# A 512-column and a 256-column product per weight tile pair become three products of 256 columns, and the copy of the low half goes

## What is computed

```python
def first_block(...):
    mod = silu(c) @ w_ada + b_ada                     # six vectors: shifts, scales, gates
    h = modulate(rmsnorm(x, g_norm_mix), sh1, sc1)
    proj = h @ w_in                                   # 2048 -> 3072
    ...                                               # convolution, gated recurrence, pooling
    x = x + gt1 * (concat([y_lru, y_pool]) @ w_out)
    h = modulate(rmsnorm(x, g_norm_ffn), sh2, sc2)
    f = (silu(h @ w_ffn_gate) * (h @ w_ffn_up)) @ w_ffn_down     # 2048 -> 5632 -> 2048
    x = x + gt2 * f
    return rmsnorm(x, g_norm_final)

def second_block(x, ...):
    h = rmsnorm_2(x, attn_norm_w)
    proj = h @ w_in                                   # 2048 -> 11264
    ...                                               # retention and block attention
    merged = sigmoid(g_ret) * (o_ret @ w_ret_up) + sigmoid(g_moba) * (o_moba @ w_moba_up)
    x = x + merged @ w_out
    up = causal_dwconv_2(rmsnorm_2(x, ffn_norm_w) @ w_ffn_up, conv_w, conv_b)
    a, b = split(up, 2)
    x = x + (silu(a) * b) @ w_ffn_down
    return rmsnorm_2(x, final_norm_w)
```

## Time and profile before

| | |
|---|---|
| time, median of 3 runs | 2662.82 us (2662.07 to 2663.64) |
| span of the profiled execution | 2662.5 us |
| TensorE matmuls busy | 2521.5 us, 95%, 14020 instructions |
| weight loads busy | 2142.7 us, 80%, 14020 |
| VectorE busy | 1904.7 us, 72%, 2383 |
| ScalarE busy | 1183.1 us, 44%, 1437 |
| granted TensorE clock, mean | 0.995 |
| granted clock at half | 426.0 to 439.6 us, and from 2648.1 on |

### The profile page before, as it was taken

How to read it: one execution, slowest core, us unless ns; L and a number is a source line. 1 busy time by engine, 2 the same in 40 slices (tenths; PEclk the granted TensorE clock), 3 DMA queues, 4 the chain that set the end, 5 groups by cost and what they waited for, 6 DMA issues and landing times.

```text
span 2662.5 us, 38962 instructions
## 1 busy us (share of the span) xinstructions
PE 2521.5 (95%) x14020; PEld 2142.7 (80%) x14020; DVE 1904.7 (72%) x2383; ACT 1183.1 (44%) x1437; POOL 9.8 (0%) x37
## 2 busy tenths in 40 slices
PE   1399998999999999999999999999999999999997
PEld 0286676888888888888888888888888888888886
DVE  7899887865555555577677565576788758875886
ACT  1154434444444444464344455455544444444443
POOL 1000000000000000000000000000000000000000
PEclk9999998999999999999999999999999999999998
DMA  9888996965555555565555455565555555565553
GB/s 359 328 314 286 341 335 231 338 214 185 186 187 183 189 184 188 162 193 180 172 177 168 160 169 191 190 183 190 180 186 185 189 180 185 182 196 182 189 170 114
DMA packets 158485, 553.91 MB, mean 208 GB/s; under 512 B 18337, under 2 KB 22433, under 8 KB 158385
## 3 DMA queue, kind: packets, MB, share of 16 engines
q1 hardware_dynamic: 156384, 549.85, 60.8%
q0 software_dynamic: 848, 2.69, 0.3%
q10 hardware_dynamic: 1152, 0.03, 0.0%
HBM read 550.38 MB, written 2.10 MB: 208 GB/s over the span
## 4 chain that ended last, share of the span: by engine, by line
PE 89%; DVE 8%; issue 2%; ACT 1%; DMA 1%; DVEq 0%; SPq 0%; ACTq 0%
PE ps L499 54%; PE ps L501 27%; DVE acc L1104 4%; PE ps L494 2%; PE ps L496 1%; PE pm L534 1%; DVE split L1060 1%; PE pm L544 1%; DMA x_t<-in_x_fm 0%; ACT split L764 0%; DVE xc L1259 0%; DVE ssq L1141 0%; PE pm L649 0%; DVE val L1175 0%; PE pm L594 0%
## 5 line engine op out<-in xcount | busy, mean ns | idle before, releaser
L1060 DVE TENSOR_TENSOR split<-raw,split 128x1024 fp32r<-128x1024 f32 (+1 forms) x864 | 1032.3, 1203 | 660.4 <-ACT split L764 658.2
L764 ACT ACTIVATE split<-raw 128x1024 fp32r<-128x1024 f32 (+1 forms) x864 | 897.7, 1043 | 1205.0 <-PE ps L501 1106.0
L499 PE MATMUL ps<-h_s,split 128*128 128x512 f32 x3904 | 1383.6, 399 | 16.1 <-DVE h_s L1169 7.2
L501 PE MATMUL ps<-h_s,split 128*128 128x256 f32 x3904 | 1094.4, 280 | 0.0
L499 PEld LDWEIGHTS ps<-h_s,split 128*128 128x128 f32 x3904 | 734.8, 188 | 208.9 <-issue 20.0
L499 PE MATMUL ps<-mid_s,split 128*128 128x512 f32 x2368 | 836.9, 399 | 0.2 <-DVE split L1060 0.2
L501 PEld LDWEIGHTS ps<-h_s,split 128*128 128x128 f32 x3904 | 738.6, 189 | 0.5
L501 PE MATMUL ps<-mid_s,split 128*128 128x256 f32 x2368 | 663.5, 280 | 0.0
L499 PEld LDWEIGHTS ps<-mid_s,split 128*128 128x128 f32 x2368 | 444.8, 188 | 121.8 <-issue 12.1
L501 PEld LDWEIGHTS ps<-mid_s,split 128*128 128x128 f32 x2368 | 446.8, 189 | 0.0
L771 ACT ACTIVATE low<-ps 128x512 f32<-128x512 f32 x224 | 129.9, 580 | 4.4 <-PE ps L501 4.4
(11 more groups left out here) (222 smaller groups left out, 1155.2 us busy)
## 6 DMA issues: line engine op xcount, KB each, us to landing
raw<-in_w_in SPq DMA_DIRECT2D x224, 512.0 KB, 3.3
ride<-in_w_ada_late SPq DMA_DIRECT2D x128, 512.0 KB, 5.6
raw<-in_w_ffn_down SPq DMA_DIRECT2D x128, 512.0 KB, 3.3
raw<-in_w_ffn_gate SPq DMA_DIRECT2D x88, 512.0 KB, 3.3
raw<-in_w_ffn_up SPq DMA_DIRECT2D x88, 512.0 KB, 3.4
raw<-in_w_ffn_a SPq DMA_DIRECT2D x88, 512.0 KB, 4.1
raw<-in_w_ffn_b SPq DMA_DIRECT2D x88, 512.0 KB, 4.4
ada<-in_w_ada SPq DMA_DIRECT2D x64, 512.0 KB, 5.8
```

The lines of the kernel that those rows point to most:

```text
L499: pe.matmul(ps[:, s, b, :], split[:, slot, k, 0, b * P:(b + 1) * P], acts[:, k0 + k, :, :].rearrange("p h t -> p (h t)"), start=start, sto ...
L501: mm = pe.matmul(ps[:, s, b, 0:T], split[:, slot, k, 1, b * P:(b + 1) * P], acts[:, k0 + k, 0, :], start=False, stop=stop)
L764: act.activation(split[:, c, 0:kt, 0, :], raw[:, CHUNKS * s + c, 0:kt, :], ACT.Copy).then_inc(hi_ready, 1)
L1060: dve.tensor_tensor(split[:, c, 0:kt, 1, :], raw[:, CHUNKS * s + c, 0:kt, :], split[:, c, 0:kt, 0, :].bitcast(F32), ALU.subtract).then_inc ...
```

## The change

Each k-tile and block now has three matmuls of 256 columns, all onto `ps[:, s, b, 0:T]`: high × high, high × low (the high weight tile again), low × high. The second half of each PSUM bank is no longer used. `copy_low`, `last_turn`, the tile `low` and the semaphore `low_copied` go, and with them the waits of ScalarE for `evacuated`. The place of `low` in SBUF stays empty, so no address moves. `evacuate` waits for `chunk_used` itself, with the count of the slab's last chunk, and reads PSUM: a copy where nothing is scaled, one multiplication where it is by rows, two (one for each block) by columns. It has one step on VectorE's own semaphore less where it scales, thus `per` falls by two.

```diff
-    low = at("low", [P, 2, 2, T], place(2 * 2 * T * 4))
+    place(2 * 2 * T * 4)
...
                 for b in range(2):
-                    if tok:
-                        pe.matmul(ps[:, s, b, :], acts[:, k0 + k, 0, b * P:(b + 1) * P],
-                                  split[:, slot, k, :, :].rearrange("p h n -> p (h n)"), start=start, stop=False)
-                        mm = pe.matmul(ps[:, s, b, 0:SLAB], acts[:, k0 + k, 1, b * P:(b + 1) * P],
-                                       split[:, slot, k, 0, :], start=False, stop=stop)
-                    else:
-                        pe.matmul(ps[:, s, b, :], split[:, slot, k, 0, b * P:(b + 1) * P],
-                                  acts[:, k0 + k, :, :].rearrange("p h t -> p (h t)"), start=start, stop=False)
-                        mm = pe.matmul(ps[:, s, b, 0:T], split[:, slot, k, 1, b * P:(b + 1) * P],
-                                       acts[:, k0 + k, 0, :], start=False, stop=stop)
+                    block = slice(b * P, (b + 1) * P)
+                    for n, (w, x) in enumerate(((0, 0), (0, 1), (1, 0))):
+                        weight, act = split[:, slot, k, w, :], acts[:, k0 + k, x, :]
+                        left, right = (act[:, block], weight) if tok else (weight[:, block], act)
+                        mm = pe.matmul(ps[:, s, b, 0:T], left, right, start=start and n == 0, stop=stop and n == 2)
             mm.then_inc(chunk_used, 1)
...
-        def copy_low(E, s, used):
-
-            act.wait_ge(chunk_used, used)
-            if not (isinstance(E, int) and E < 2):
-                act.wait_ge(evacuated, E - 1)
-            act.activation(low[:, s, :, :], ps[:, s, :, T:2 * T], ACT.Copy).then_inc(low_copied, 1)
...
-            S = 2 * pair + s
-            copy_low(S + offset[0], s, CHUNKS * S + CHUNKS)
...
-        def evacuate(E, s, dst, scale=None):
-
-            dve.wait_ge(low_copied, E + 1)
-            both = low[:, s, :, :]
+        def evacuate(E, s, dst, used, scale=None):
+
+            dve.wait_ge(chunk_used, used)
             if scale is None:
-                ins = dve.tensor_tensor(dst, ps[:, s, :, 0:T], both, ALU.add)
+                ins = dve.tensor_copy(dst, ps[:, s, :, 0:T])
+            elif scale == "columns":
+                for b in range(2):
+                    ins = dve.tensor_scalar(dst[:, b, :], ps[:, s, b, 0:T], rstd_col[:, b:b + 1], None, ALU.mult)
             else:
-                own(dve.tensor_tensor(both, ps[:, s, :, 0:T], both, ALU.add))
-                if scale == "columns":
-                    for b in range(2):
-                        ins = dve.tensor_scalar(dst[:, b, :], both[:, b, :], rstd_col[:, b:b + 1], None, ALU.mult)
-                else:
-                    ins = dve.tensor_tensor(dst, both, scale[:, :].unsqueeze(1).to_broadcast([P, 2, T]), ALU.mult)
+                ins = dve.tensor_tensor(dst, ps[:, s, :, 0:T], scale[:, :].unsqueeze(1).to_broadcast([P, 2, T]), ALU.mult)
             ins.then_inc(evacuated, 1)
             dve.wait_ge(evacuated, E + 1)
...
-                per = 1 if first == S_FFN else 2 * (CONV_2 - 1) + 4
+                per = 1 if first == S_FFN else 2 * (CONV_2 - 1) + 2
```

More of the change, by code:

```diff
@@ L261, in build @@
     chunk_used = sem("chunk_used")
-    low_copied = sem("low_copied")
     evacuated = sem("evacuated")
@@ L764, in convert @@
             act.activation(split[:, c, 0:kt, 0, :], raw[:, CHUNKS * s + c, 0:kt, :], ACT.Copy).then_inc(hi_ready, 1)
-        def copy_low(E, s, used):
-            act.wait_ge(chunk_used, used)
-            if not (isinstance(E, int) and E < 2):
-                act.wait_ge(evacuated, E - 1)
-            act.activation(low[:, s, :, :], ps[:, s, :, T:2 * T], ACT.Copy).then_inc(low_copied, 1)
-        offset = [0]
         def turn(pair, s, mid=None, kt_next=KT):
@@ L783, in turn @@
                     mid(c)
-            S = 2 * pair + s
-            copy_low(S + offset[0], s, CHUNKS * S + CHUNKS)
-        def last_turn(pair, s):
-            S = 2 * pair + s
-            copy_low(S + offset[0], s, CHUNKS * S + CHUNKS)
         def turn_rows(S, c):
@@ L960, in ffn @@
                             square(n_sq, q - 1)
-                            last_turn((down + q) // 2, q % 2)
                     square(n_sq, OUT_SLABS - 1, pre)
@@ L1033, in _ @@
                     convert(pair + 1, 0, c)
-                if c == 1:
-                    copy_low(S_MERGE + 2 * m, 0, CHUNKS * (S_MERGE + m) + 2)
-            copy_low(S_MERGE + 2 * m + 1, 1, CHUNKS * (S_MERGE + m) + 4)
             act.wait_ge(merged_t, m + 1)
             act.activation(h_s[:, 2 * m:2 * m + 2, 0, :], val[:, 0, :, :], ACT.Copy).then_inc(merged_hi, 1)
-        offset[0] = OUT_SLABS
         pre_2 = (3, mid_s, col("ffn_norm_w_2", 0, DB))
@@ L1088, in turn @@
                     mid(c)
-            evacuate(2 * pair + s + offset[0], s, dst, scale)
+            S = 2 * pair + s
+            evacuate(S + offset[0], s, dst, CHUNKS * S + CHUNKS, scale)
         def add_ada(part, k, first, piece, loaded, times, added):
@@ L1400, in residual_turn @@
                 both(1)
-                evacuate(2 * pair + s + offset[0], s, val[:, s, :, :])
+                evacuate(2 * pair + s + offset[0], s, val[:, s, :, :], CHUNKS * (2 * pair + s) + CHUNKS)
             else:
@@ L1668, in _ @@
                         dve.wait_ge(merged_ready, m)
-                    evacuate(S_MERGE + 2 * m, 0, val[:, 0, :, :])
+                    evacuate(S_MERGE + 2 * m, 0, val[:, 0, :, :], CHUNKS * (S_MERGE + m) + 2)
                     own(dve.tensor_tensor(val[:, 0, :, :], val[:, 0, :, :], sig_r[:, 2 * m:2 * m + 2, :], ALU.mult))
-            evacuate(S_MERGE + 2 * m + 1, 1, val[:, 1, :, :])
+            evacuate(S_MERGE + 2 * m + 1, 1, val[:, 1, :, :], CHUNKS * (S_MERGE + m) + 4)
             own(dve.tensor_tensor(val[:, 1, :, :], val[:, 1, :, :], sig_m[:, 2 * m:2 * m + 2, :], ALU.mult))
```

## The result

| | before | after |
|---|---|---|
| time, median | 2663.2 us (2662.1 to 2664.9) | 2716.3 us (2714.6 to 2717.5) |
| ratio to before, 95% interval | | 1.0199 (1.0186 to 1.0212) |
| span of the profiled execution | 2662.5 us | 2715.7 us |

The change costs 53 us, 2.0%. The forecast was 2650; the range (2600 to 2775) holds the time, the direction was wrong. The time lies outside the likeliest case's own bounds (2610 to 2679); the range holds it because it was drawn round rival one's 2768.

A forecast was written before the change was run, and what follows sets the result against it. The prediction took the spacing of TensorE's matmuls as the bound: 2662.5 us, less 10.9 for TensorE and 1.5 for VectorE and ScalarE, gave 2650.1, stated as 2650, with a range of 2600 to 2775.

The forecast's parts named there:

- the likeliest case: Whole kernel: the forecast of 2650 us with the bounds of both its parts, 2610 to 2679; chance 0.50.
- rival one: Weight product on TensorE: every load costs a fixed 15.7 ns, a triple 367.2 ns, +107 us, 2768 us; chance 0.22.
- What bounds the kernel: Whole kernel: TensorE's matmul spacing sets the time, 89% of the chain; VectorE and ScalarE savings count only where TensorE waits.
- The TensorE part: Weight product: three 256-column steps of 116.6 ns, 349.9 for a pair's 351.5, -10.9 us over 6784; bounds -48 to +17.
- A load fits under a 256-column step: Weight product on TensorE: a load of 0.113 us hides under a 116.6 ns step with some 4 ns to spare.
- The slow supply: TensorE instruction supply: a load with its matmul due every 117 ns may come too slowly, 0 to +180 us; chance 0.05.
- Rival two: Weight product on TensorE: 256-column steps alone settle at the load's 0.113 us, a triple 339 ns, -85 us, 2576; chance 0.12.
- Rival three: TensorE's loop turns: larger bodies fetch instructions again, 1.4 us in each of 58 turns, +78 us, 2728 us; chance 0.06.
- Rival four: Weight product: the second load of the same high tile is left out, 349.9 ns a triple; no chance of its own.
- The VectorE and ScalarE parts: Evacuation and low copy: ScalarE loses 130 us, VectorE 60, nearly all off the path; -1.5 us, bounds -1 to -5.
- the cover: Each slab's evacuation: the 0.58 us low copy runs beneath a 1.2 us VectorE convert; if that failed, 130 us.
- The last down group: Before the last down products: TensorE waits 1.74 us for hidden values; one addition less gives back 0.68 us.

The follow-up runs named there:

- only the split: Kernel before with its 512-column product issued as two of 256, low copy and old evacuation kept: 2717.9 us, ratio 1.0198.

## Why the prediction was wrong, by its own steps

**What bounds the kernel: right.** The spacing of TensorE's matmuls set the time and little else counted.

**The TensorE part: the direction was lost here.** The step that failed is "I take what the trace shows of such a step: 3 × 116.6". The 116.6 ns was the recorded step of a 256-column matmul between 512-column ones. In a series of its own it is 120.0: 8.5 ns a triple more than the pair instead of 1.6 less, + 57.7 us where the sum had - 10.9. The error was to split a pair of 351.5 ns into two costs, 234.8 and 116.6, at the recorded start between them. The run with 384 + 128 + 256 columns shows that such a split can be off by 50 ns (170 for 120, 60 for 111.5). The two uniform series give the costs, 226.7 + 120.0 = 346.7 ns, and that is the pair of the faster rhythm (346.9); the slower rhythm adds 6.7 to it. The pair's mean of 351.5 is a mix of the two.

**"A load fits under a 256-column step": right, and no help.** The floor seen in series is 111.5 ns, and the one-column matmuls had shown it well enough (113). But 13.3 ns stand beside the columns although the floor lies under the step.

**Rival one came nearest, mis-sized.** It had a fixed time for every load; the runs show one for every matmul with its whole load, without telling which of the two has it. It said 15.7 ns, taken from the mean pair (31.5 / 2), and 2768 us. The faster rhythm (26.9 / 2 = 13.4, worked out in the same paragraph) was the right source: 13.3. Three of these and 320 ns of columns are 360.0, and with this the rival's own sum gives 2719 for the 2716 measured. Its own deciding point, a 256-column step over 117.5 ns, was met at 120.0. Both arguments against it fell. The excess of the 512-column step being twice that of the 256-column one came from the recorded split; in series of their own both have 13.3. And that the half clock shows no excess is true and says nothing of the upper clock; after the change the row is

```profile
440.61 3.62 PE L496 MATMUL ps<-h_s,split 128*128 128x256 f32 x16
```

(3.62 - 0.41) / 15 = 0.214 us, the bare columns at 1.2 GHz, in a kernel that has 13.3 ns more at 2.4. The Trainium skill (TensorE: Matmul & The Clock Gate, "Back-to-back issue gap") has the same asymmetry: N/1.2 cold with nothing added, N/2.4 and a constant warm; only the constant differs.

**The slow supply: no.** Steps of 111.5 ns were seen with a load each, below the 117 and the 126 ns of that case. They are below 124 ns too, what the prediction's estimate by the Trainium skill (TensorE: Matmul & The Clock Gate, Part 2) makes of a matmul and a load at 62 ns each; 62 ns for the matmul alone no run here tests.

**Rival two: no.** The steps did not lock to the load; they do that only below about 235 columns (111.5 - 13.3 = 98.2 ns of columns), an estimate from the rows of 192 and 256 columns, with no run between them.

**Rival three: no.** The instruction queue brought 92 blocks for 63, so the program did grow. But the list of TensorE's waits has no entry that recurs in the 58 turns, from 569 to 1215 us not one step of the product is over 122 ns, and from 1608 to 2635 one is. The Trainium skill (Runtime: NRT & Kernel Launch, "Instruction fetch mechanics") has a rule by which a body of 384 could stall at each turn, and the trace shows none.

**Rival four: no.** 20,804 loads and as many matmuls: nothing was left out.

**The VectorE and ScalarE parts: right in place, one size off.** The copy was put at the upper end, 0.68; measured 0.684. The column-scaled reads were put at 0.41 to 0.42; measured 0.477, 1 us in all on an engine with room. The low copy is gone and the cover held. Busy time: VectorE - 54 for - 60 (the column-scaled reads and the converts took longer), ScalarE - 108 for - 130 (the overlap above). The end: from the start of the last product matmul to the next matmul it was 3.87 us and is 3.25, the 0.6 that was forecast. The wait before the last evacuation, which was to show it, is only 0.31 us shorter, because VectorE had finished what came before 0.3 us earlier against the last matmul. The last down group: - 0.96 for - 0.68; with only the split TensorE's wait there was 1.50 us, so 0.72 of it is the evacuation's. In all the long steps gave back 2.4 us, where 1.5 was taken and the bounds were 1 to 5.

**Chances.** 0.50 stood on the mean of a step in a mix. The prediction named in its last sentence that the trace held no 256-column step behind another one; a term with no row of its own should have weighed more in the chances, with 360 ns (the faster rhythm's excess for each load) as a case at least as likely as 350.

**What stays open.** What in the engine makes up the 13.3 ns is not known, nor that it is a fixed cost. The steady steps 113.3, 120.0, 173.3 and 226.7 ns and the pairs 346.7 and 353.3 are all whole multiples of 6.67 ns, the time of 16 columns (17, 18, 26, 34, 52 and 53 of them), while the uneven ones (111.5, 117.7, 230.0 on the mean) are not. The widths tried are multiples of 16 columns too, so 13.3 ns can't be told from any excess over 6.7 ns that is rounded up to this grid; a width off it was not run. The excess does not depend on the columns (256, 384, 512), goes to 6.7 with half a load under 256 columns, is gone at 1.2 GHz, and grows irregularly with small loads under 512. Nor is it known why a mixed series has two rhythms 6.7 ns apart and what chooses between them. The experiments show what a series costs, not the mechanism beneath.

## What to carry to other kernels

Where each matmul brings its own weight load, its count costs as well as its columns: at the upper clock each took its columns and 13.3 ns more here (from 256 columns up, with whole loads), so a product of 512 columns is cheaper than two of 256 by that much, and cutting it pays only if it frees over 13.3 ns of TensorE's own time elsewhere. Don't price a matmul by the recorded start of its neighbour in a mix of widths; price the repeating group, or look for a series of that one width. An evacuation made simpler on engines that are idle a quarter of the time or more returns nearly nothing.

## What the runs showed of the hardware that was not expected

- Uniform series of matmuls, each with a whole 128-column load, at 2.4 GHz: 226.7 ns (512 columns), 173.3 (384), 120.0 (256), 111.5 (192 and 128 alike). At 1.2 GHz: 213 for 256 and for 128 columns.
- 512 and 256 columns in turn have two stable rhythms, 346.7 and 353.3 ns a pair. Two profiled executions of one kernel differ by 11.3 us in span and by 1.9 ns a pair, 13 us, so it is the share of each rhythm that sets them apart; that kernel's times lay between 2654 and 2671 us.
- The order of the same matmuls is worth 0.6%: wide, wide, narrow, narrow against wide, narrow, wide, narrow.
- Smaller loads are no cheaper by rule: under 256 columns 120.0, 113.3 and 117.7 ns with 128, 64 and 32 weight columns, under 512 columns 226.7, 230.0 and 231.4.
- VectorE's operation on 256 elements out of PSUM by a column pointer took 477 ns, from SBUF 350; that of 512 elements took 684 whether it copied, added or multiplied.
